# Ordering work around the end of sparse attention: the first head's cosine product goes ahead of weight work on POOL, and two panels of the next mixer run inside the last two heads and across the barrier

## The reference, cut to what matters

```python
proj = h @ w_in
...
a_q = apply_partial_rope(rms_norm_2(a_q...), cos, sin)      # 8 heads of 128
s = einsum(q, k) * scale, masked to the indexer's top 128 keys, softmax, einsum(p, v)
...
qkv = silu(causal_short_conv(g_qkv, conv_w))                # per head: q, k, v columns of proj
gq, gk = l2_normalize(...)
o_gdn = gated_delta_rule_chunked(gq, gk, gv, g, beta)
```

## Time and profile before

| | |
|---|---|
| Median of 3 runs | 1680.46 us (1679.95 to 1680.67) |
| Profiled execution, its own time | 1685.93 us |
| Its span in the trace | 1684.1 us |
| PE busy, share of the span | 1624.3 us, 96% |
| DVE, ACT, POOL busy | 974.9, 686.8, 241.8 us |
| Mean granted clock of PE | 0.984 |

### The profile page before, as it was taken

One profiled execution on the slowest core, in us unless ns is written; L12 is line 12 of the kernel. 1 busy time (PEld: TensorE's weight loads), 2 busy tenths in 40 slices (PEclk: granted clock), 3 DMA queues, 4 the chain that ended last, 5 costly groups with the idle time before them and its releaser, 6 DMA issues.

```text
span 1684.1 us, 24685 instructions
## 1 busy us (share of the span) xinstructions
PE 1624.3 (96%) x9418; PEld 1302.3 (77%) x9418; DVE 974.9 (58%) x1500; ACT 686.8 (41%) x1040; POOL 241.8 (14%) x222
## 2 busy tenths in 40 slices
PE   6999979999999999999799999999999999999998
PEld 3777768888888887667457888878787888888887
DVE  5556545444444457788476768586775544444443
ACT  5455544423232355424455445363553432323232
POOL 0233430000000033143200402204050000000000
PEclk7999989999999999999899999999999999999999
DMA  4222213333333334223103122131221333333333
GB/s 132 76 64 63 76 38 88 101 100 88 100 99 100 88 99 120 63 70 84 37 1 102 50 76 76 50 86 40 79 65 38 88 100 89 103 96 100 89 101 99
DMA packets 258166, 135.19 MB, mean 80 GB/s; under 512 B 10699, under 2 KB 254940, under 8 KB 258068
## 3 DMA queue, kind: packets, MB, share of 16 engines
q1 hardware_dynamic: 258068, 133.84, 28.3%
HBM read 131.64 MB, written 2.18 MB: 79 GB/s over the span
## 4 chain that ended last, share of the span: by engine, by line
PE 78%; DVE 9%; issue 7%; ACT 4%; POOL 1%; DMA 0%; PEldq 0%; ACTq 0%; POOLq 0%; DVEq 0%; SPq 0%; PEld 0%
PE bank L231 18%; PE bank L233 18%; PE bank L232 18%; PE bank L1692 4%; PE bank L493 4%; PE bank L495 3%; PE bank L494 3%; DVE arena L1997 2%; DVE w_lo L215 2%; ACT w_hi L211 2%; PE bank L1272 1%; PE bank L1526 1%; PE bank L1708 1%; PE bank L1745 1%; PE bank L508 1%
## 5 line engine op out<-in xcount | busy, mean ns | idle before, releaser
L211 ACT CAST w_hi<-raw 128x1024 fp32r<-128x1024 f32 x234 | 245.2, 1048 | 301.6 <-PE bank L233 271.6
L231 PE MATMUL bank<-m_hi,w_hi 128*128 128x512 f32 x856 | 336.3, 393 | 3.8 <-POOL w_lo L221 2.8
L233 PE MATMUL bank<-m_hi,w_lo 128*128 128x512 f32 x856 | 333.2, 389 | 0.0
L232 PE MATMUL bank<-m_lo,w_hi 128*128 128x512 f32 x856 | 333.1, 389 | 0.0
L215 DVE TENSOR_TENSOR w_lo<-raw,w_hi 128x1024 fp32r<-128x1024 f32 x218 | 271.1, 1244 | 98.7 <-ACT w_hi L211 97.8
L231 PE MATMUL bank<-h_hi,w_hi 128*128 128x512 f32 x640 | 254.5, 398 | 9.1 <-DVE w_lo L215 4.6
L232 PE MATMUL bank<-h_lo,w_hi 128*128 128x512 f32 x640 | 251.5, 393 | 0.0
L233 PE MATMUL bank<-h_hi,w_lo 128*128 128x512 f32 x640 | 251.4, 393 | 0.0
L231 PEld LDWEIGHTS bank<-m_hi,w_hi 128*128 128x128 f32 x856 | 160.8, 188 | 40.9 <-issue 3.4
L232 PEld LDWEIGHTS bank<-m_lo,w_hi 128*128 128x128 f32 x856 | 160.8, 188 | 34.2 <-issue 1.2
L233 PEld LDWEIGHTS bank<-m_hi,w_lo 128*128 128x128 f32 x856 | 160.7, 188 | 33.6
(11 more groups left out here) (282 smaller groups left out, 2269.1 us busy)
## 6 DMA issues: line engine op xcount, KB each, us to landing
raw<-in_l_w_ff SPq DMA_DIRECT2D x64, 512.0 KB, 3.9
raw<-in_w_in SPq DMA_DIRECT2D x64, 512.0 KB, 3.8
raw<-in_w_mlp_up SPq DMA_DIRECT2D x32, 512.0 KB, 4.0
raw<-in_w_mlp_down SPq DMA_DIRECT2D x32, 512.0 KB, 4.1
raw<-in_l_w_in SPq DMA_DIRECT2D x24, 512.0 KB, 3.8
raw<-in_l_w_out SPq DMA_DIRECT2D x8, 512.0 KB, 4.1
arena<-gb_rows SPq DMA_DIRECT2D x16, 256.0 KB, 4.4
raw<-in_w_out SPq DMA_DIRECT2D x8, 512.0 KB, 4.1
```

Source lines behind the costliest of these rows:

```text
L211: act.copy(w_hi[q.par][:], raw[q.par][:]).then_inc(s["w_hi_ready"], 1)
L231: pe.matmul(g_bank[q.par][:], w_hi[q.par][:, k], hi[:, k], start=(k == 0), stop=False)
L232: pe.matmul(g_bank[q.par][:], w_hi[q.par][:, k], lo[:, k], start=False, stop=False)
L233: last = pe.matmul(g_bank[q.par][:], w_lo[q.par][:, k], hi[:, k], start=False, stop=(k == KT - 1))
```

## The change

It does five things.

1. POOL's cosine product of head 0 stands ahead of the low part of panel u = 24, and that of head 1 ahead of u = 25. The loop of `pool_att` starts at head 2. DVE writes head 1's normalised queries before it works on head 0's rope.
2. The first GDN panel's 24 products run in two halves, inside heads 6 and 7, between `spread` and `values`. The transposes that used to go to the same bank go to the rope's bank `b[5]` in these two heads.
3. ACT rounds the second GDN panel's weights in head 6, behind the exponentials of head 7; DVE makes its low part behind the output of head 6. In head 6, DVE's `normal` of head 7 stands ahead of that output.
4. PE runs the second GDN panel after it has reported to the barrier and before it waits for it.
5. ACT's table load stands ahead of the barrier.

```diff
             for u in range(13, 17):
                 pool_split(pool, Panel(N_IN1, 0, 0, u))
-            for u in range(17, 9 + 2 * ATT_H + 1):
+            for u in range(17, 9 + 2 * ATT_H - 1):
                 pool_split(pool, Panel(N_IN1, 0, 0, u))
+            for i in range(2):
+                att_rope(pool, i, i)
+                pool_split(pool, Panel(N_IN1, 0, 0, 8 + 2 * ATT_H + i))
+
+        def att_rope(pool, i, e):
+            pool.wait_ge(s["r_y"], i + 3)
+            pool_rope(pool, i + 7, aq[:, e], ca)
...
+        gdn_first = [Panel(N_GDN, 10, 0, u) for u in range(2)]
+
+        def turned_at(i, k):
+            bk, o = t_at[k]
+            return (b[5] if i >= ATT_H - 2 and bk is g_bank[gdn_first[0].par] else bk), o
...
                 spread(i, e)
                 if i + 3 < ATT_H:
                     pe_turn(pe, i + 3, 1 - e)
+                if i >= ATT_H - 2:
+                    for k in range(KT // 2):
+                        pe_eighth(pe, gdn_first[0], KT // 2 * (i - ATT_H + 2) + k, *lay_in[1])
                 values(i, e)
...
                 if 0 < i < ATT_H - 1:
                     act_exponentials(act, i + 1, 1 - i % 2)
+                if i == ATT_H - 2:
+                    act_split(act, gdn_first[1])
+            tanh_tables(act)
...
             queries(0)
+            queries(1)
             dve_rope(dve, 7, aq[:, 0], sa)
-            queries(1)
             scores(0, 0)
...
+                if i == ATT_H - 2:
+                    normal(i + 1, (i + 1) % 2)
                 output(i)
-                if i + 1 < ATT_H:
+                if i == ATT_H - 2:
+                    dve.wait_ge(s["w_ready"], N_GDN + 3)
+                    dve_split(dve, gdn_first[1])
+                if i < ATT_H - 2:
                     normal(i + 1, (i + 1) % 2)
...
             pe_att(pe)
-            fence(pe, 3)
+            pe.drain().then_inc(s["phase_done"], 1)
+            pe_panel(pe, gdn_first[1], *lay_in[1])
+            pe.wait_ge(s["phase_done"], 12)
             pe_gdn(pe)
```

More of the change, by code:

```diff
@@ L1513, in spread @@
                 pe.wait_ge(s["pn_r"], TT * i + TT)
+                if i == ATT_H - 2:
+                    pe.wait_ge(s["rp_ss"], ATT_H + 7)
                 for k in K_ORDER:
-                    bk, o = t_at[k]
+                    bk, o = turned_at(i, k)
                     for q in range(k, TT):
@@ L1610, in pool_att @@
         def pool_att(pool):
-            with pool.Fori(0, HPK) as j:
+            with pool.Fori(1, HPK) as j:
                 for e in range(2):
-                    i = 2 * j + e
-                    pool.wait_ge(s["r_y"], i + 3)
-                    pool_rope(pool, i + 7, aq[:, e], ca)
+                    att_rope(pool, 2 * j + e, e)
         at[0] = 0
@@ L1717, in panels @@
                 for u in range(10):
-                    if u == 0 and p or u == 5:
+                    if p == 0 and u < 2:
+                        pass
+                    elif u == 0 or u == 5:
                         for k in range(KT):
@@ L1922, in panels @@
                     tanh_tables(act)
-                else:
-                    act_split(act, gdn_panel(p, 1))
                 for u in range(6):
@@ L1969, in small @@
                 log_tables(act)
-            tanh_tables(act)
             for p in range(PAIRS):
@@ L2094, in panels @@
                         out_add(p - 1, e)
-                else:
-                    dve_split(dve, gdn_panel(p, 1))
                 for u in range(6):
@@ L2174, in small @@
                                                          b[2 * e + 1][:, 0:P], ALU.mult, ALU.add).then_inc(s["st2"], 1)
-            dve.wait_ge(s["w_ready"], N_GDN + 3)
             for p in range(PAIRS):
```

## The result

The median is 1670.85 us (1669.58 to 1671.94, 5 runs) against 1680.67 us before; the ratio is 0.9931 with a 95% interval of 0.9920 to 0.9942, so 11.6 us (9.7 to 13.4) faster. The two medians alone differ by 9.8 us: of the five executions of the kernel before, three lie near 1680 and two near 1685, and the ratio counts them all. The forecast was 14.6 us faster and 1665.9 us, in a range from 1662 to 1672.

What follows compares the result with a forecast made beforehand. PE, busy 96% of the span, was taken to bound the kernel, gaining only through idle and low clock. Terms -10.3 + 1.2 - 5.5 = -14.6 us, off the median before, gave 1665.9 us, range 1662 to 1672.

Steps and rivals of the forecast that it cites:

- the forecast's own mechanism: All three terms hold (head 0's scores, last heads, conv chain): chance 0.76, own range 1663 to 1669 us.
- the lead is lost at the barrier: Rival: first convolution starts no earlier against the barrier, fourth panel's load late or chain held elsewhere; 1671.4 us, chance 0.12.
- the named signs of being wrong: PE idle over 2 us before head 0's scores, ACT's second rounding waiting for a load, low clock in heads 6 and 7.
- The first term, 10.3 us: Before head 0's scores: earlier cosine product removes 7.16 us of PE idle and 3.16 us of low clock.
- The sums' cover: Head 0's rope sum ends near 804.7, PE's scores can start at 806.8: cover 2.1 us, or 1.3 if held.
- The heads, +1.2 us: Panel one inside heads 6 and 7 delays the barrier's release by 1.2 us, bounds +0.7 and +1.7.
- The conv chain, -5.5 us: Behind the barrier, ACT's first copy comes at release + 0.35, first tanh at + 6.2 instead of + 11.7; 5.1 to 5.7 us gained.
- What is late next is the load of the fourth panel ... Cover 0.3 to 1.9 us: Issued behind the broadcasts at release + 1.8, landing in 3.7 to 5.3 us, before ACT wants it at + 7.4.
- The table load, 1.28 us without its place: At the barrier: ACT's table load, hidden before, would now cost 1.28 us unless moved ahead of the barrier.
- PE's lead of 6.1 us: Across the barrier: PE ends panel two at release + 4.8 instead of + 10.9; surplus returns as waits at sums of squares.
- the last rival: Same or slower as the clock falls in heads 6 and 7: 1681.6 us (0.03), or 1687 with panel three slow (0.02).
- The falling clock: Rival: PE's changes of bank and work in heads 6 and 7 bring the low clock, +15.7 us; chance 0.05.

Runs made afterwards that it cites:

- e2: Kernel before with only POOL's cosine products of heads 0 and 1 put earlier and DVE's queries of head 1 earlier; ratio 0.9949 (0.9935 to 0.9963).
- e3: Changed kernel with the cosine-product and query reordering undone, leaving the panels in the last heads and across the barrier; ratio 0.9989 (0.9980 to 0.9998).
- e8: e1 with DVE's divisions for head 7 behind head 6's output again; ratio 0.9917 (0.9901 to 0.9934), median 1669.41 us.
- e1: Changed kernel with the fourth GDN panel's load issued ahead of the barrier and the four row broadcasts; ratio 0.9907 (0.9893 to 0.9921).
- e4: Like e1, but the fourth panel's load is issued behind the barrier, directly ahead of the four broadcasts; ratio 0.9910 (0.9896 to 0.9924).
- e9: e1 with ACT's table load behind the barrier again; ratio 0.9922 (0.9904 to 0.9941), median 1668.93 us.
- e6: e1 with PE's second GDN panel behind the barrier instead of across it; ratio 0.9919 (0.9902 to 0.9935), median 1669.09 us.
- e10: The changed kernel run and profiled again, nothing altered; ratio 0.9925 (0.9911 to 0.9938), median 1670.2 us.

## Why the prediction was right, and where its size was off

The median, 1670.85 us, lies in the stated range, but 5 us above the forecast of 1665.9, outside the 1663 to 1669 that the forecast's own mechanism was given, and nearest to the 1671.4 of the rival "the lead is lost at the barrier". One of the named signs of being wrong came true: ACT's second rounding behind the barrier waits for a load, 3.26 us. So two of the three terms held, the third failed for a bit over half, and that the time is in the range is owed to its width. Of the 5 us, 2.6 are the sum's (below). The rest fits the start: the forecast subtracted from a median of three, 1680.46, where the rounds of the experiments have medians of 1682.7 to 1683.2 us for the kernel before.

- **The first term, 10.3 us: right in the trace.** e2, this part alone, is 10.25 us shorter from O to the barrier. That the two agree so closely is partly luck of the profile: both are read against the same execution of the kernel before, in which the low clock behind the gap cost 3.1 us; in e3's it cost 1.6. By the ratio over several executions this part gives 8.6 us (6.2 to 10.9). The sums' cover was smaller than I wrote, since DVE's sum took 1.25 us beside POOL's low part: it ended at 804.82, 1.3 us ahead of the scores, not 2.1. By the Trainium skill (SBUF — State Buffer, Who interferes with whom) a DVE instruction with two SBUF inputs contends with a GpSimd one that reads SBUF, and the order of issue decides which of them is held. The trace agrees: POOL's low part started first, at 801.88, the sum at 803.57 took 1.25 us, and the 1.3 us are what that rule gave. The small tensor_scalar was held too (2.25 us), and ACT was through 0.95 us before PE's panel ended, where I had said 1.0.
- **The heads, +1.2 us: +0.7.** O to T is 77.69 us with the panels and 76.97 without (e2), so 0.7 us, the lower bound. No idle, and clock 1.00, as forecast. e8 shows that DVE's reorder is what holds this: without it the idle and the low clock are back, 4.0 us in its trace.
- **The conv chain, -5.5 us: right on the mechanism, wrong in what it yields here.** The first copy came at T + 0.23 and the first tanh at T + 6.16 (forecast 0.35 and 6.2). But T to the second convolution went from 18.02 to 15.60, 2.4 us and not 5.5. The step that failed is "What is late next is the load of the fourth panel ... Cover 0.3 to 1.9 us". The issue was right (T + 1.81). The landing was taken from the earlier trace rows, 3.7 to 5.3 us, in which no load stands directly behind the broadcasts: in the kernel before even the fourth panel's waits for a low part behind the barrier, is issued 2.4 us behind the last broadcast (886.97, T + 3.7) and lands in 4.7 us. Here it was issued 0.5 us behind the last broadcast and took 8.7 us. So the load landed at T + 10.5, and 3.1 us of the term were lost. e1 and e4, which move this load alone, give them back: 5.51 us from T to the second convolution, and 15.0 us in all. The rival "the lead is lost at the barrier" named this mechanism, with all of the lead lost; a bit over half of it was.
- **The table load, 1.28 us without its place: 1.05 us** (e9, on e1). I did not test it in the changed kernel; there the wait for the load of 3.3 us stands behind it, so I estimate that it would have been covered.
- **PE's lead of 6.1 us, "surplus" over the chain: right as far as it was tried.** e6 takes away PE's start across the barrier, 0.8 us of the lead, and nothing changes. So this part of the change gives nothing here, on e1. That panel one inside the heads and the early split of panel two are what counts is argued from the chain; neither was taken out by itself.
- **The sum.** 10.3 - 0.7 + 2.4 = 12.0 us, the trace's 11.96. The forecast of 14.6 was 2.6 us too much: 3.1 too much in the chain, 0.5 too little in the heads. (The 1687 us of the last rival would be 0.4% above the kernel before; the prediction writes 0.2%.)
- **The falling clock: out.** PE changes banks and kinds through heads 6 and 7 at 1.00 in every version without an idle gap; in e8, with one of 2.18 us, it falls. An idle gap of that length doesn't always bring it down: behind the 2.27 us in which PE waits for the late load in the kernel after, and the 2.47 us in e10, the clock stays at 1.00, while in e3, behind 2.63 us at the same place, it is 0.50 for the next 3 us.

## What to carry to other kernels

When a chain is made to start earlier, look up the transfer that it will meet next, and take its landing time from a place with the same neighbours in the queue, not from the spread of all loads; a load whose condition is already met belongs ahead of the barrier and of bulk transfers. A small product of an engine that serves as a helper should not stand behind bulk work that is itself waiting for a third engine: here one low part of 2.4 us, started 4.9 us after POOL was free, cost PE 7 us and then 1.6 to 3 us of low clock. Work moved into gaps pays where it lets the engines that follow start sooner; that PE itself is ahead is worth nothing while it follows another chain.

## What the runs showed of the hardware that I had not expected

- A 512 KB load issued directly behind four 256 KB row broadcasts took 8.7 us to land (8.9 in e10, 9.0 in e3), against 3.7 to 5.3 us. Issued 1.8 us earlier, in front of them, it took 4.4 us (e4). A load issued 2.1 us behind the last broadcast took 6.2 us (e1), and 2.4 us behind it 4.7 and 4.1 us (before, e2).
- Beside POOL's low part, DVE's tensor_scalar of 128x4 took 2.25 us; in the kernel before it takes 0.17 us where POOL is idle. Beside the second of two DVE products (1.41 us for both, two inputs each), POOL's cosine product took 1.74 us, against 1.26.
- The low clock behind an idle of 7.2 us cost 3.1 us in the profile of the kernel before and 1.6 us in that of e3, for the same work.
- The clock also fell where PE had hardly been idle: in the kernel before it is 0.57 from 970 to 974, with no idle over 0.6 us in the 15 us ahead, and 1.00 at the same place in the kernel after.
